# A ninth place for rotating expert chunks, the last norm's rows spread by matmuls, and the order of experts found by matmuls, in a two-block transformer kernel

## The chip, the cores and the metric

The kernel runs on one core of a Trainium2 chip. The metric is the device time of one execution in microseconds (us). Engines in what follows: PE (TensorE), PEld (its weight loads), DVE (VectorE), ACT (ScalarE), POOL (GpSimd), SP (SyncE, which issues most DMA transfers).

## The reference, cut to what matters

Two transformer blocks for 256 tokens of width 1024, in float32. The first (attention beside retention, then a dense feed-forward) is not touched. The second adds 16 meta tokens, runs a gated delta rule beside a stick-breaking attention, merges the two branches, and ends in a mixture of experts and a layer norm:

```python
def second_block(...):
    ...
    mix = hybrid_mixer(h, ...)                    # ends in merged @ w_out
    h = layer_norm_2(ALPHA * h + mix, ln1_g, ln1_b)
    ffn = hierarchical_moe(h, ...)
    h = layer_norm_2(ALPHA * h + ffn, ln2_g, ln2_b)
    return h[:, N_META:]

def hierarchical_moe(h, ...):                     # 4 groups of 8 experts, EXPERT_FF = 256
    g_idx = argmax(softmax(t @ router_group_w + b)); ...
    top_logit, top_idx = top_k(logits of that group, 2)
    for every expert e:                           # weights 1024x256, 1024x256, 256x1024
        hid = silu(t @ w_gate[e]) * (t @ w_up[e]) * combine[:, e]
        y += hid @ w_down[e]
```

Each token uses 2 of the 32 experts, but all experts' weights are read: 48 chunks of 2 MiB.

## The kernel before, in words

Everything is one program with a hand-written order on each engine. Weights reach SBUF in chunks of 2 MiB (128 partitions x 4096 floats), numbered in the order in which they are used. `used` is a semaphore that PE raises by one for each chunk it has done with. SP walks through the chunks: for chunk n it waits until the chunk that held the same place before is used, then issues the transfer; each place has its own `landed` semaphore. Up to the experts there are 5 places in `ring`. In the expert stage (chunks 49 to 96) three more in `scr` join, SLOTS = 8: chunk 49 + m goes to place m mod 8, so it waits for chunk n-8. The first five are ring places as they come free, then the three of scr.

A gate chunk holds one expert's gate and up weights, a down chunk those of two experts. Experts 0 to 5 are fixed (chunks 49 to 57, read by number, `in_stream`), the 26 others are ranked by how many tokens chose them, and SP reads the number of the expert from the table `perm` (`in_gates`, `in_downs`). PE works through eleven groups p = 0 to 10 of 2 or 4 experts: gates 49, 50 and down 51; 52, 53, 54; 55, 56, 57; 58 to 61 with 62, 63; 64, 65, 66; 67 to 70 with 71, 72 (p = 5); 73, 74, 75 (p = 6); 76 to 79, 80, 81; 82, 83, 84; 85 to 88 with 89, 90 (p = 9); 91 to 94 with 95, 96 (p = 10). The rows of a group's tokens are gathered from DRAM (POOL, `hrows`), turned by PE (L1341), multiplied with the gates (L1361, `gate_up`), by ACT and DVE made into the hidden rows, turned (L1374), multiplied with the down weights (L1415) and added into PSUM banks 4 to 7 by a product with a selection matrix (L1383, `scatter`; L1395 the last).

`keep_warm` (L2008) is a filler: products of constants into a bank that nobody reads. In `gate_up` three of them stand between the waits for the gates of a group of four from p = 7 on (L1351 to L1354).

Chunks 57 and 58 (PIECED) take the places of 49 and 50, piece by piece as group 0's products proceed (`pieces`, L1876 to L1887; semaphore `d_mm`, L1365).

Ahead of the experts: `mgd` counts the four parts of the merged branches. Then comes the output product (w_out2, chunks 47 and 48), the norm, the router (L1289), and on DVE the choice (L1548 to L1580). PE counts tokens by expert (L1295 to L1299, `lg_mm` 2), DVE makes each token's place, `flag` (whether an expert has too many tokens, then a dense branch runs that is not the case here) and `first`, the matrix that selects group 0's rows (L1594). `rank_experts` and `order_experts` then build on DVE, on all 128 partitions and over 26x26 comparisons, the rank of each expert and `perm`.

The last norm's gain and shift are spread over the 128 partitions by a transfer of 1 MiB into `rowB[:, 1]` (`rows(5, 1, ...)` in `pool_tail`).

Of the kernel before, what the change touches and what calls it, by code (L numbers as in the profile page):

```python
# [13 lines left out]
P = 128  # L14
# [110 lines left out]
def _consts():  # L125
    n = 0
    for name, k in (("ident", P), ("ones", P), ("causal", P), ("decay", RH * P), ("xi", 2 * P), ("zeta", RH),
                    ("inv", RDK // 2), ("ucum", P), ("strict", P), ("m16", P), ("off16", P), ("causT", P),
                    ("sbmul", P), ("sbadd", P), ("ntri", P), ("neg", 1), ("tie", 8), ("iota", 3 * P), ("tid", T), ("code", NE), ("tier", NE - 6), ("rank", NE - 6), ("order", NE - 6), ("gstart", 12), ("eye32", 32)):
        CONST[name] = (n, k)  # L130
        n += k
    CONST["end"] = (n, 0)
# [8 lines left out]
def const_array():  # L141
# [39 lines left out]
    put("order", order[None, :])  # L181
    put("gstart", 1 + 128 * np.arange(12)[None, :])
# [3 lines left out]
def build(nc, IN, out):  # L186

    ctx = ExitStack()
    with ctx:
        def sb(name, shape, dt=F32):  # L190
# [10 lines left out]
            cT cTv cB_mm cB_ev eg eu hid d_mm rt_e rt_x in_rt ug R_mm E01 ex01 kvn_tr kv_ev  # L201
            gram ab rd_mm rd_v rd_a u_mm uv wv s_mm sv vn_mm vn_v o_mm o_v os orv on on_tr
# [3 lines left out]
        landed = [S.landed0, S.landed1, S.landed2, S.landed3, S.landed4, S.landed5, S.landed6, S.landed7]  # L206
# [269 lines left out]
        def pe_second(pe, mm, transposes, out_proj, keep_warm):  # L476
# [17 lines left out]
            for g, (n, m, form) in enumerate(GROUPS):  # L494
# [33 lines left out]
                if g == 20:  # L528
                    pe.wait_ge(S.ug, 1)
                    pe.wait_ge(S.nr, 8)  # L530
                    for b in range(2):
                        mm(b_(4 + b), C("ones"), M2[:, 512 * b:512 * b + 512], start=True, stop=True)
                    mm(psum[:, 6, 0:64], C("ones")[0:META, :], M2[0:META, 1024:1088], start=True, stop=True)\
                        .then_inc(S.R_mm, 1)
# [180 lines left out]
            pe.wait_ge(S.wv, 1)  # L715
# [86 lines left out]
        def act_second(act, link, ln_sqrt, act_hT):  # L802
# [78 lines left out]
            sc.copy(M3[:, 0:1024], psum[:, 3:5, :].rearrange("p a b -> p (a b)")).then_inc(S.wv, 1)  # L881
# [36 lines left out]
        def dve_second(dve, v, link, chain, residual, normalise, to_hT, proj_wait):  # L918
# [54 lines left out]
            dve.wait_ge(S.R_mm, 1)  # L973
# [220 lines left out]
        def pool_tail(pool, link, affine, rows):  # L1194
# [5 lines left out]
            rows(5, 1, S.in_row1)  # L1200
# [14 lines left out]

        lay = gnB[:, :, :].rearrange("p a b -> p (a b)")
# [26 lines left out]
        ranks, low, rise, order, key, over = (arena(408 + RANKED * n, RANKED) for n in range(6))  # L1243
        above = scr[:, 5408:5408 + RANKED * RANKED].rearrange("p (a b) -> p a b", a=RANKED)
# [27 lines left out]
        SLOTS = RING + 3  # L1272
        LATE = 6
        extra_slot = [arena(6944 + CH * n, CH) for n in range(SLOTS - RING)]
# [5 lines left out]
        def pe_experts(pe, mm, transposes, keep_warm):  # L1280
# [18 lines left out]
            mm(psum[:, 5, 2 * NE:3 * NE], C("ones"), mem[:, 1, :], start=False, stop=True).then_inc(S.lg_mm, 1)  # L1299
            keep_warm(6, 2)  # L1300
            pe.wait_ge(S.flag, 1)
            crowded = pe.value_load(flag[0:1, 0:1], min_val=0, max_val=1)
            with pe.If(crowded == 0):
                pe_gathered(pe, mm, keep_warm)
            with pe.Else():
                pe_dense(pe, mm)

        def pe_gathered(pe, mm, keep_warm):

            pe.wait_ge(S.cmb, 2)  # L1310
# [7 lines left out]
            pe.wait_ge(S.cmb, 3)  # L1318
# [26 lines left out]
            def gate_up(p):  # L1345
# [12 lines left out]
                for k in range(KD):  # L1358
                    for i, e in enumerate(group):
                        weights = ring_at(GATE[e]).rearrange("p (k n) -> p k n", k=KD)  # L1360
                        last = mm(psum[i * w:(i + 1) * w, 2, :], xg[p % 2][:, k, i * w:(i + 1) * w],  # L1361
                                  weights[:, k, :], start=(k == 0), stop=(k == KD - 1))
# [35 lines left out]
            def down(p):  # L1398
# [9 lines left out]
                for half in range(2):  # L1408
                    if p == NP - 1:
                        landed_wait(pe, DOWN[group[2 * half]])  # L1410
                    for f in range(2):
                        for i, e in enumerate(group):
                            weights = ring_at(DOWN[e]).rearrange("p (e f n) -> p e f n", e=2, f=2)
                            c = f * P + i * w
                            last = mm(psum[i * w:(i + 1) * w, half, :], turned[p % 2][:, c:c + w],  # L1415
                                      weights[:, e % 2, f, half * 512:(half + 1) * 512], start=(f == 0), stop=(f == 1))
# [5 lines left out]
            for p in range(NP):  # L1422
# [9 lines left out]
                if LATE <= p < NP - 1:  # L1432
                    add_x(p - LATE)
                    scatter(p)
            for half in range(2):
                last_scatter(half)

        def pe_dense(pe, mm):

            pe.wait_ge(S.cmb, 3)  # L1440
# [5 lines left out]
            def down(s):  # L1446
# [6 lines left out]
                w = ring_at(n).rearrange("p (e f n) -> p e f n", e=2, f=2)  # L1453
                for f in range(2):
                    for t in range(T):
                        for half in range(2):
                            last = mm(b_(4 + 2 * t + half), hid[:, s % 4, f * NT + t * P:f * NT + (t + 1) * P],
                                      w[:, e % 2, f, half * 512:(half + 1) * 512],
# [3 lines left out]
            def gate_up(s):  # L1462
# [8 lines left out]
                w = ring_at(n).rearrange("p (k w n) -> p k w n", w=2, k=KD)  # L1471
                for i in range(2):
                    for f in range(2):
                        for k in range(KD):
                            last = mm(psum[:, 2 * (e % 2) + i, f * NT:(f + 1) * NT],
                                      w[:, k, i, f * P:(f + 1) * P], hT[:, k, META:L2],
# [1423 lines left out]
```

## Time and profile before

| | |
|---|---|
| median of 3 runs | 943.24 us (942.4 to 943.26) |
| the profiled execution's own time | 943.65 us |
| its span, first to last instruction | 941.8 us |
| mean granted TensorE clock | 0.986 |
| PE / PEld busy | 889.5 / 557.5 us |
| DVE / ACT / POOL busy | 367.2 / 174.3 / 92.3 us |
| moved by DMA | 219.29 MB |

Times in rows are from the span's start. Busy time of PE is modelled from pipelined records and says little of a limit by itself. A float32 product of PE shows as two records. "idle before <-X" is how long an engine stood before an instruction and what released it. In the last quarter of the span the DMA engines are busy without a break, and PE nearly so.

### The profile page before, as it was taken

To read this page: it belongs to the slowest core of one execution; us is meant where nothing else is said; L and a number is where in the kernel's file an instruction comes from. 1 tells how busy PE (TensorE), PEld (TensorE's weight loads), DVE (VectorE), ACT (ScalarE), POOL (GpSimd) and SP (SyncE) were. 2 spreads that over 40 slices of the span, in tenths; PEclk is the share of its full clock that TensorE was granted. 3 is DMA by queue.
4 is the path that set the end of the run, shared out by engine and by line. 5 is a ranking of instruction groups with operands and counts; after the bars stand their busy time and mean duration, and the time that the engine had idled before them with its cause. 6 is when DMAs were issued, how large, how long until landed. Compare 5 with 4: busy or idle time off the path is not lost.

```text
span 941.8 us, 11299 instructions
## 1 busy us (share of the span) xinstructions
PE 889.5 (94%) x4615; PEld 557.5 (59%) x4615; DVE 367.2 (39%) x834; ACT 174.3 (19%) x359; POOL 92.3 (10%) x91
## 2 busy tenths in 40 slices
PE   6999899999999998999999999999999996899985
PEld 3446756776667663688779898577455332343331
DVE  5746816433323339363475221662256111111014
ACT  3126512100000001222241221350111100000001
POOL 0045303301101100300000000000122000000000
PEclk9999999999999999999999999999999998999998
DMA  9997847544334553033352022202597999999993
GB/s 368 431 422 280 343 182 296 196 178 179 143 137 168 200 203 134 1 136 132 127 219 103 1 90 95 85 8 90 205 393 289 386 425 423 428 420 427 424 415 135
DMA packets 22617, 219.29 MB, mean 233 GB/s; under 512 B 3297, under 2 KB 3569, under 8 KB 8098
## 3 DMA queue, kind: packets, MB, share of 16 engines
q1 hardware_dynamic: 19186, 205.76, 54.6%
q0 software_dynamic: 3376, 12.76, 3.6%
q8 instruction: 38, 0.62, 0.3%
q14 instruction: 17, 0.14, 0.0%
HBM read 219.69 MB, written 2.10 MB: 235 GB/s over the span
## 4 chain that ended last, share of the span: by engine, by line
PE 82%; DVE 7%; DMA 7%; ACT 2%; issue 1%; SPq 0%; DVEq 0%; ACTq 0%
PE psum L2276 12%; PE psum L2298 9%; PE psum L508 8%; PE psum L1361 8%; PE psum L463 6%; DMA scr<-in_gates 4%; PE psum L2064 4%; PE psum L1415 3%; PE psum L755 3%; PE psum L1383 3%; PE psum L2257 3%; PE psum L2036 3%; PE psum L582 3%; DMA ring<-in_stream 2%; PE psum L2008 2%
## 5 line engine op out<-in xcount | busy, mean ns | idle before, releaser
L2276 PE MATMUL psum<-hT,ring 128*128 128x256 f32 x512 | 115.4, 379 | 1.1 <-issue 1.1
L2276 PEld LDWEIGHTS psum<-hT,ring 128*128 128x128 f32 x512 | 97.1, 190 | 26.7 <-issue 14.2
L1361 PE MATMUL psum<-ring,hT 128*32 128x512 f32 (+1 forms) x352 | 73.8, 617 | 13.7 <-DMA scr<-in_gates 11.0
L508 PE MATMUL psum<-hT,ring 128*128 128x272 f32 x320 | 74.2, 393 | 0.0
L508 PEld LDWEIGHTS psum<-hT,ring 128*128 128x128 f32 x320 | 60.6, 190 | 12.9 <-issue 0.5
L2298 PE MATMUL psum<-scr 128*128 128x512 f32 x128 | 59.5, 592 | 0.0
L2737 DVE TENSOR_TENSOR scr<-ring 128x512 f32<-128x512 f32 x16 | 11.1, 691 | 121.6 <-PE psum L2298 121.6
L463 PE MATMUL psum<-hT,ring 128*128 128x256 f32 x256 | 57.8, 382 | 0.0
L1361 PEld LDWEIGHTS psum<-ring,hT 128*32 128x32 f32 (+1 forms) x352 | 21.5, 125 | 58.0 <-issue 55.2
L2064 PE MATMUL psum<-ring,hT 128*128 128x512 f32 (+1 forms) x128 | 53.1, 574 | 2.4 <-ACT hT L2369 2.4
L1747 DVE TENSOR_TENSOR scr<-psum,scr 128x256 f32<-128x256 f32 x11 | 4.7, 424 | 127.4 <-ACT scr L1520 127.4
L463 PEld LDWEIGHTS psum<-hT,ring 128*128 128x128 f32 x256 | 47.8, 190 | 6.6 <-issue 0.2
L2298 PE MATMUL psum<-ring,scr 128*128 128x512 f32 x96 | 46.2, 592 | 0.0
L2462 ACT ACTIVATE scr<-psum 128x256 f32<-128x256 f32 x32 | 12.3, 383 | 171.0 <-PE psum L2276 171.0
L1361 PE MATMUL psum<-scr,hT 128*32 128x512 f32 (+1 forms) x160 | 43.7, 603 | 0.0
L2064 PEld LDWEIGHTS psum<-ring,hT 128*128 128x128 f32 x128 | 24.1, 190 | 31.0 <-issue 31.0
L2298 PEld LDWEIGHTS psum<-scr 128*128 128x128 f32 x128 | 24.3, 190 | 24.6 <-issue 23.9
L2008 PE MATMUL psum<-cst 128*128 128x512 f32 x80 | 36.8, 606 | 0.0
L1383 PE MATMUL psum<-rowB,scr 128*128 128x512 f32 x80 | 36.3, 596 | 0.0
L1996 POOL TENSOR_TENSOR scr<-scr 128x256 f32<-128x256 f32 x32 | 20.5, 642 | 156.8 <-ACT scr L2462 156.8
L755 PE MATMUL psum<-scr,ring 128*128 128x256 f32 x128 | 29.1, 383 | 0.0
L582 PE MATMUL psum<-scr 128*128 128x128 f32 (+1 forms) x272 | 27.8, 253 | 0.7 <-ACT scr L870 0.4
(526 smaller groups left out, 1234.2 us busy)
## 6 DMA issues: line engine op xcount, KB each, us to landing
ring<-in_stream SPq DMA_DIRECT2D x54, 2048.0 KB, 9.2
ring<-in_gates SPq DMA_DIRECT2D x17, 2048.0 KB, 18.2
scr<-in_gates SPq DMA_DIRECT2D x8, 2048.0 KB, 23.5
ring<-in_downs SPq DMA_DIRECT2D x12, 1024.0 KB, 17.8
scr<-in_downs SPq DMA_DIRECT2D x10, 1024.0 KB, 22.8
rowB<-in_rows POOLq DMA_DIRECT2D x6, 1024.0 KB, 9.9
scr<-in_stream SPq DMA_DIRECT2D x3, 2048.0 KB, 18.4
scr<-in_downs SPq DMA_DIRECT2D x8, 512.0 KB, 15.2
```

What stands on the lines that cost most here:

```text
L463: last = mm(o, w[:, k, (i % 4) * P:(i % 4 + 1) * P], hT[:, k, META:L2], start=(k == 0), stop=(k == KD - 1))
L508: last = mm(psum[:, g % 4, 0:L2], w[:, k, m * P:(m + 1) * P], hT[:, k, :], start=(k == 0), stop=(k == KD - 1))
L582: last = mm(o, prob(lhsT, p), prob(rhs, p), start=True, stop=True)
L755: last = mm(o, w[:, k, m * P:(m + 1) * P], src[:, k, :], start=(k == 0), stop=(k == 3))
L1361: last = mm(psum[i * w:(i + 1) * w, 2, :], xg[p % 2][:, k, i * w:(i + 1) * w], weights[:, k, :], start=(k == 0), stop=(k == KD - 1))
L1383: last = mm(b_(4 + 2 * t + half), scat[p % 2][:, t * P:(t + 1) * P], yg[p % 2][:, half * 512:(half + 1) * 512], start=(p == 0), stop=False)
L1415: last = mm(psum[i * w:(i + 1) * w, half, :], turned[p % 2][:, c:c + w], weights[:, e % 2, f, half * 512:(half + 1) * 512], start=(f == 0) ...
L2008: mm(psum[:, bank, 0:width], C("ident"), C("ones", 0, 1).broadcast_to([P, width]), start=True, stop=True)
L2036: last = mm(b_(4 + 2 * t + half), src[:, k, t * P:(t + 1) * P], w[:, k, :], start=(k == 0), stop=(k == KD - 1))
L2064: return mm(psum[:, 2 * c + t, 0:b - a], hT[:, k, tok(t)], ring_at(AT["head"] + k)[:, 2048 + a:2048 + b], start=(k == 0), stop=(k == KD - 1))
L2276: last = mm(psum[:, f if f < 4 else 0, 0:NT], w[:, k, m * P:(m + 1) * P], hT[:, k, META:L2], start=(k == 0), stop=(k == KD - 1))
L2298: last = mm(b_(i), lhsT, rhs, start=(j == 0), stop=(j == FT // 2 - 1))
```

## The change

1. **A ninth place.** SLOTS is 9. The new place is made of three stretches of tables that nobody reads any more in the expert stage: `rowB[:, 1]` (4 of 8 blocks of 512 floats), constants (3), the upper half of `gnB` (1). A chunk in it is loaded by three transfers, and `block_of` finds a block of it. The places are filled in another order: three of the ring, then the three of scr and the new one, then the last two of the ring; ahead of the first scr place SP waits for `mgd` 4. Chunk n waits for n-9. The pieced chunks are 58 and 59, both read by `perm`.
2. **The last norm's rows by PE.** Since `rowB[:, 1]` is taken, the rows come as 8x256 floats into a dead constant. PE spreads them by products with a column of the identity, 256 columns at a time, two to a round into bank 3, and ACT copies each round to scr; four rounds, after group 9's scatter.
3. **Order of experts.** Two small products give the counts as a column; DVE compares on 26 partitions; two more products turn ranks into the order. `perm` is written before the branch, and the two functions on DVE go.
4. Some semaphores are merged into others that already exist, to make room for `landed8`.

```diff
-        SLOTS = RING + 3
+        WHOLE = RING + 3
+        SLOTS = WHOLE + 1
+        GAINS_AT = NP - 2
+        last_rows = arena(1824, 2, DM)
...
+        turns = freed[:RING - 2] + list(range(RING, SLOTS)) + freed[RING - 2:]
         for m in range(AT["end"] - AT["experts"]):
-            slot_of[AT["experts"] + m] = m % SLOTS if m % SLOTS >= RING else freed[m % SLOTS]
+            slot_of[AT["experts"] + m] = turns[m % SLOTS]
...
+        in_parts = ((rowB[:, 1, :, :].rearrange("p a b -> p (a b)"), 0, 4), (cst[:, 256:1792], 4, 7),
+                    (lay[:, 512:1024], 7, 8))
...
+                sp.wait_ge(S.perm, 1)
+                first_gate, second_gate = expert(gate_of[a]), expert(gate_of[b])
                 for i, (lo, hi) in enumerate(SLOT_PIECES):
...
+                if n == AT["experts"] + RING - 2:
+                    sp.wait_ge(S.mgd, 4)
                 if n < FIXED_END:
-                    sp.dma_start(ring_at(n), IN["stream"][n]).then_inc(landed[slots[n]], 16)
+                    for words, a, b in parts(n):
+                        sp.dma_start(words, IN["stream"][n][:, a * 512:b * 512]).then_inc(landed[slots[n]], 16)
...
-            rows(5, 1, S.in_row1)
+            pool.dma_start(gain_rows, IN["rows"][5].rearrange("a (b n) -> (a b) n", n=NT)).then_inc(S.in_row1, 16)
...
+            for t in range(T):
+                last = mm(psum[0:RANKED, 5, 3 * NE:3 * NE + 1], mem[:, t, FIXED:NE], C("ones", 0, 1),
+                          start=(t == 0), stop=(t == T - 1))
+            last.then_inc(S.lg_mm, 1)
             keep_warm(6, 2)
+            pe.wait_ge(S.cmb, 2)
+            number = C("num")[0:RANKED, 0:1]
+            mm(psum[0:1, 5, ORDER_AT:ORDER_AT + RANKED], number, at_rank, start=True, stop=True)
+            mm(psum[:, 5, RANKS_AT:RANKS_AT + RANKED], C("ones")[0:RANKED, :], rank_diag, start=True, stop=True)\
+                .then_inc(S.lg_mm, 1)
+
+            def last_gains(q):
+
+                pe.wait_ge(S.in_row1, 48)
+                if q:
+                    pe.wait_ge(S.gains_v, q)
+                for c in range(2):
+                    j = 2 * q + c
+                    last = mm(psum[:, 3, c * NT:(c + 1) * NT], C("ident")[0:8, j:j + 1].broadcast_to([8, P]), gain_rows,
+                              start=True, stop=True)
+                last.then_inc(S.gains, 1)
...
+                if p == GAINS_AT + 1:
+                    pe.wait_ge(S.gains_v, 4)
...
                 if LATE <= p < NP - 1:
                     add_x(p - LATE)
                     scatter(p)
+                if p == GAINS_AT:
+                    for q in range(4):
+                        last_gains(q)
...
+        def gains_out(act, q):
+            act.wait_ge(S.gains, q + 1)
+            nc.scalar.copy(last_rows[:, q // 2, q % 2 * 512:(q % 2 + 1) * 512], b_(3)).then_inc(S.gains_v, 1)
...
+            v.scalar_tensor_tensor(key, psum[:, 5, 2 * NE + FIXED:3 * NE], 64.0, C("tier"), ALU.mult, ALU.add)
+            v.scalar_tensor_tensor(key_col, psum[0:RANKED, 5, 3 * NE:3 * NE + 1], 64.0, C("num")[0:RANKED, 1:2],
+                                   ALU.mult, ALU.add)
             link(places_prefix(v, C("code")))
+            v.tensor_scalar(above, key[0:RANKED, :], key_col, None, ALU.is_gt)
             v.tensor_reduce(many, over, AX, ALU.add)
             link(places_member(v))
+            v.tensor_reduce(rank_col, above, AX, ALU.add)
             v.tensor_scalar(many, many, BIG + 0.5, None, ALU.is_gt)
             link(places_sum(v))
+            v.tensor_scalar(at_rank, C("rank")[0:RANKED, :], rank_col, None, ALU.is_equal)
+            v.tensor_scalar(rank_diag, C("ident")[0:RANKED, 0:RANKED], rank_col, None, ALU.mult).then_inc(S.cmb, 1)
...
+            dve.wait_ge(S.lg_mm, 3)
+            v.tensor_copy(ranks, psum[:, 5, RANKS_AT:RANKS_AT + RANKED])
+            order = psum[0:1, 5, ORDER_AT:ORDER_AT + RANKED]
+            link(v.tensor_tensor(low[0:1, :], C("order")[0:1, :], order, ALU.subtract))
+            v.scalar_tensor_tensor(perm[0:1, :], low[0:1, :], crowd[0:1, :], order, ALU.mult, ALU.add).then_inc(S.perm, 1)
```

SP, at the entry of the expert stage. The operand left of the arrow is the place (`ring`, `scr`, or in the kernel after `rowB`, `cst`, `gnB`). Before:

```order
L1911 DMA ring<-in_stream 128x4096 x52
L1911 DMA scr<-in_stream 128x4096 x3
L1882 DMA ring<-in_stream 128x1024
L1872 TENSOR_LOAD perm
L1872 ISA x2
L1886 ISA
L1886 DMA ring<-in_gates 128x1024
```

And now:

```order
L1966 DMA ring<-in_stream 128x4096 x50
L1966 DMA scr<-in_stream 128x4096 x3
L1966 DMA rowB<-in_stream 128x2048
L1966 DMA cst<-in_stream 128x1536
L1966 DMA gnB<-in_stream 128x512
L1966 DMA ring<-in_stream 128x4096 x2
L1925 TENSOR_LOAD perm
L1925 ISA x2
L1925 TENSOR_LOAD perm
L1925 ISA x2
```

Two ring chunks moved behind the scr places and the three-part chunk, and both reads of `perm` stand ahead of the first piece.

DVE, from the counts to the branch. Before:

```order
L1583 TENSOR_SCALAR scr<-psum 128x26
L1664 TENSOR_TENSOR scr<-psum,cst 128x64
L1585 TENSOR_REDUCE scr<-scr 128x1
L1669 TENSOR_TENSOR scr<-scr 128x64 x2
L1587 TENSOR_SCALAR scr<-scr 128x1
L1674 TENSOR_REDUCE scr<-scr 128x4
L1589 SCALAR_TENSOR_TENSOR scr<-scr 128x1
L1590 CAST flag<-scr 128x1
```

And now:

```order
L1625 SCALAR_TENSOR_TENSOR scr<-psum,cst 128x26
L1626 SCALAR_TENSOR_TENSOR scr<-psum,cst 26x1
L1704 TENSOR_TENSOR scr<-psum,cst 128x64
L1629 TENSOR_SCALAR scr<-scr 26x26
L1630 TENSOR_REDUCE scr<-scr 128x1
L1709 TENSOR_TENSOR scr<-scr 128x64 x2
L1632 TENSOR_REDUCE scr<-scr 26x1
L1633 TENSOR_SCALAR scr<-scr 128x1
L1714 TENSOR_REDUCE scr<-scr 128x4
L1635 TENSOR_SCALAR scr<-cst,scr 26x26
L1636 TENSOR_SCALAR scr<-cst,scr 26x26
L1637 SCALAR_TENSOR_TENSOR scr<-scr 128x1
```

Six small operations have come in between those that lead to `flag` and `first`.

PE, between group 9's down products and group 10's gate products. Before:

```order
L1415 MATMUL psum<-ring,scr 32x512 x16
L1334 MATMUL psum<-X,gnB 128x512
L1383 MATMUL psum<-rowB,scr 128x512 x4
L2008 MATMUL psum<-cst 128x512 x9
L1361 MATMUL psum<-ring,hT 32x512 x3
```

And now:

```order
L1446 MATMUL psum<-scr 32x512 x16
L1365 MATMUL psum<-X,gnB 128x512
L1415 MATMUL psum<-rowB,scr 128x512 x4
L1326 MATMUL psum<-cst 128x256 x8
L2070 MATMUL psum<-cst 128x512 x9
L1391 MATMUL psum<-rowB,hT 32x512
```

The eight products of 256 columns stand ahead of the filler, whose nine are still all there.

## Rows read from the trace of the kernel before

**Rows 1.** Table by stage: stretch, length, busy time by engine, granted clock, DMA share, GB/s.
```profile
660.00:680.00 20.00, 20.00 (x52) 9.05 (x51) 4.77 (x9) 0.29 (x1) 1.06 (x2) 1.00 0.54 208
700.00:720.00 20.00, 18.61 (x104) 11.00 (x102) 12.68 (x44) 2.55 (x5) 2.76 (x2) 0.91 0.72 276
740.00:900.00 160.00, 145.72 (x758) 54.24 (x758) 20.13 (x40) 13.25 (x24) 4.94 (x5) 0.97 1.01 421
```

**Rows 2.** Chain that ended last: start, length, what.
```profile
711.99 7.02 PE psum L1361 x32
...
796.69 8.39 PE psum L1361 x64
...
813.57 2.68 issue
816.25 8.78 PE psum L1361 x32
...
924.63 0.43 DVE scr L1753
...
925.11 3.64 PE psum L1415 x32
```

**Rows 3.** Waits of PE, 700 to 942 us: total, times, longest.
```profile
PE psum L1361 <- DMA scr<-in_gates: 11.0, 2, 9.0
```

**Rows 4.** Line L1916, the issues at 782.2 us (chunk 73) and 788.4 us (chunk 74).
```profile
L1916 SPq DMA_DIRECT2D ring<-in_gates x1: 338/338/338, 782.2 to 782.2; - x1
...
DMA to landing us min/median/max: 29.0/29.0/29.0
...
L1916 SPq DMA_DIRECT2D ring<-in_gates x1: 337/337/337, 788.4 to 788.4; - x1
...
DMA to landing us min/median/max: 27.7/27.7/27.7
```

**Rows 5.** Timeline of PE: start, length, instruction, idle before and its releaser.
```profile
710.14 1.84 PE L1321 MATMUL psum<-cst,scr 128*128 128x1 f32 x16
...
906.15 7.92 PE L2008 MATMUL psum<-cst 128*128 128x512 f32 x18
916.04 0.63 PE L1361 MATMUL psum<-ring,hT 128*32 128x512 f32 x3 [1.98 <-DMA scr<-in_gates]
```

**Rows 6.** Timeline of POOL.
```profile
660.76 1.06 POOL L1938 DMA_DIRECT2D rowB<-in_rows  x2 [43.77 <-DVE scr L1182]
```

**Rows 7.** Timeline of SP's queue.
```profile
687.76 2.61 SPq L1911 DMA_DIRECT2D scr<-in_stream  x3
713.89 0.33 SPq L1882 DMA_DIRECT2D ring<-in_stream  x1
716.70 0.35 SPq L1886 DMA_DIRECT2D ring<-in_gates  x1
```

**Rows 8.** The page's DMA issues: count, KB each, median us to landing.
```profile
ring<-in_downs SPq DMA_DIRECT2D x12, 1024.0 KB, 17.8
```

**Rows 9.** Timeline of DVE.
```profile
703.07 0.17 DVE L1583 TENSOR_SCALAR scr<-psum 128x26 f32<-128x26 f32 x1
703.16 0.21 DVE L1664 TENSOR_TENSOR scr<-psum,cst 128x64 f32<-128x64 f32 x1
...
715.40 0.31 DVE L1610 SCALAR_TENSOR_TENSOR perm<-scr 128x26 int32<-128x26 f32 x1
...
719.56 0.42 DVE L1747 TENSOR_TENSOR scr<-psum,scr 128x256 f32<-128x256 f32 x1 [2.71 <-ACT scr L1520]
```

**Rows 10.** Table by stage in steps of 2 us (columns as in rows 1).
```profile
816.00:818.00 2.00, 1.75 (x6) 0.76 (x8) 0.00 (x0) 0.00 (x0) 0.00 (x0) 0.62 1.03 430
...
922.00:924.00 2.00, 1.12 (x12) 0.13 (x4) 0.32 (x1) 0.38 (x1) 0.00 (x0) 1.00 0.70 264
```

**Rows 11.** The page's costliest groups: busy us, mean ns.
```profile
L2276 PE MATMUL psum<-hT,ring 128*128 128x256 f32 x512 | 115.4, 379 | 1.1 <-issue 1.1
```

**Rows 12.** Line L1513, ACT's copies of 128x512: ns min/median/max.
```profile
L1513 ACT COPY hT<-psum x11: 585/586/587, 710.3 to 896.7; 128x512 f32<-128x512 f32 x11
```

More of the change, by code:

```diff
@@ L1242, in build @@
         crowd, many = arena(908, 1), arena(909, 1)
-        ranks, low, rise, order, key, over = (arena(408 + RANKED * n, RANKED) for n in range(6))
-        above = scr[:, 5408:5408 + RANKED * RANKED].rearrange("p (a b) -> p a b", a=RANKED)
+        ranks, low, rise, key, over = (arena(408 + RANKED * n, RANKED) for n in range(5))
+        above, at_rank, rank_diag = (scr[0:RANKED, 5408 + RANKED * n:5408 + RANKED * (n + 1)] for n in range(3))
+        key_col, rank_col = scr[0:RANKED, 5488:5489], scr[0:RANKED, 5489:5490]
+        ORDER_AT, RANKS_AT = 3 * NE + 32, 4 * NE + 32
         perm = sb("perm", [P, RANKED], I32)
@@ L1434, in pe_gathered @@
                     scatter(p)
+                if p == GAINS_AT:
+                    for q in range(4):
+                        last_gains(q)
             for half in range(2):
@@ L1531, in act_gathered @@
                     .then_inc(S.yv if p < NP - 1 else S.xgv, 1)
+                if p == GAINS_AT:
+                    for q in range(4):
+                        gains_out(act, q)
         def act_dense(act):
@@ L1543, in act_dense @@
                 nc.scalar.activation(eg_s[:, e % 2, :], b_(2 * (e % 2)), ACT.Silu).then_inc(S.eg, 1)
+            for q in range(4):
+                gains_out(act, q)
         def dve_experts(dve, v, link, chain, residual, normalise):
@@ L1881, in pieces @@
                         sp.wait_ge(S.used, AT["experts"] + 2)
-                    sp.dma_start(ring_at(a)[:, lo:hi], IN["stream"][a][:, lo:hi]).then_inc(landed[slots[a]], 16)
-                    if i == 0:
-                        sp.wait_ge(S.perm, 1)
-                        g = expert(gate_of[b])
-                    sp.dma_start(ring_at(b)[:, lo:hi], IN["gates"][bass.ds(g, 1), :, lo:hi])\
-                        .then_inc(landed[slots[b]], 16)
+                    for n, g in ((a, first_gate), (b, second_gate)):
+                        sp.dma_start(ring_at(n)[:, lo:hi], IN["gates"][bass.ds(g, 1), :, lo:hi])\
+                            .then_inc(landed[slots[n]], 16)
             def last_downs():
@@ L1915, in _ @@
                 elif n in gate_of:
-                    sp.dma_start(ring_at(n), IN["gates"][bass.ds(expert(gate_of[n]), 1)]).then_inc(landed[slots[n]], 16)
+                    g = expert(gate_of[n])
+                    for words, a, b in parts(n):
+                        sp.dma_start(words, IN["gates"][bass.ds(g, 1), :, a * 512:b * 512]).then_inc(landed[slots[n]], 16)
                 else:
                     for half in range(2):
-                        sp.dma_start(ring_at(n)[:, half * (CH // 2):(half + 1) * (CH // 2)],
-                                     IN["downs"][bass.ds(expert(down_of[n] + half), 1)]).then_inc(landed[slots[n]], 16)
+                        g = expert(down_of[n] + half)
+                        for words, a, b in parts(n):
+                            lo, hi = max(a, 4 * half), min(b, 4 * half + 4)
+                            if lo < hi:
+                                sp.dma_start(words[:, (lo - a) * 512:(hi - a) * 512],
+                                             IN["downs"][bass.ds(g, 1), :, (lo - 4 * half) * 512:(hi - 4 * half) * 512])\
+                                    .then_inc(landed[slots[n]], 16)
             for n in range(2 * T):
```

94 lines of the change are left out of this document (43 added, 51 removed).

## The prediction, made before the changed kernel ran

> **What bounds the kernel now.** I read four views in this order. First the table by stage [rows 1]: from 740 us to 900 us the core's DMA share is 1.01 and the rate 421 GB/s, while PE is also nearly always busy. At 660 to 680 us the share is only 0.54. So the expert stage is a stream of 2 MiB chunks of weights at full rate. Second, the chain that ended last [rows 2]: after group 5's products (from 796.69 us) it has a stand of 2.68 us at 813.57, and from 816.25 on it is PE's own work. Third, the waits of PE: PE's gate products waited for a transfer 11.0 us in two places, 9.0 and 2.0 [rows 3]. Fourth, the landings [rows 4]: chunk 73 landed at 782.2 + 29.0 = 811.2 us, chunk 74 at 788.4 + 27.7 = 816.1 (so one step of the stream is 4.9 us), which is where PE, free since 813.57, starts group 6's gate products (816.25). The last gate, 94, landed at 916.0 [rows 5], and one step of the stream before it, at about 911.0, gate 93.
>
> The lesson is in PE's own rows at the end [rows 5]. Between 816.25 and 914.07 PE never waits for a weight (the second wait above is the one at 914). The filler of 7.92 us at 906.15 is not a wait: it is 9 matmuls in three sets of three, between the waits for the gates of the last group, and it is issued whether the gates are there or not. So the real wait for the last gate is 1.98 us [rows 5]. Stream and PE end within 2 us of each other, and making the stream alone earlier by more than that moves PE only through the place where PE last hung on the stream, chunk 74.
>
> **The ninth place.** Chunk n now waits for chunk n-9 to be used, before for n-8; the first chunk that waits for the expert stage to begin is 58 instead of 57. As everything else in the pattern is the same, chunk n+1 should land when chunk n did: 74 at 811.2 instead of 816.1, 94 at 911.0 instead of 916.0. That needs the stream to be full throughout, which [rows 1] show, and the nine chunks to be in before they are wanted: four of them now leave once the merged branches are formed (S.mgd 4, on which POOL's transfer of 660.76 us waited too [rows 6]) instead of from 687.76 on [rows 7], into a stretch that is half empty [rows 1]: from 661 us to the first gate products at 711.99 [rows 2] there is room for ten steps of 4.9 us, and the DMA share shows that not all of it is used. In SP's order of after the four are the three to scr and the one in three parts. The 1 MiB of gain and shift rows that is no longer read (half a chunk, 2.5 us of the stream) lies in the same stretch and gives nothing.
>
> The pieces of the ninth place go as three transfers (8, 6 and 2 KiB per partition) instead of one. In the trace the down chunks already go in two transfers each [rows 8] inside a stream that holds 421 GB/s, so I take 0, with at most 0.3 us for each of the five such chunks as an outer bound.
>
> **The start of the stream.** Order of experts: on PE two products of 26x1 are added ahead of the counts' signal. The nearest row is 16 records of 128x1 in 1.84 us [rows 5], 0.115 us each, so 4 records = 0.46 us. On DVE six small operations come in before `first`. Neighbours that don't wait for each other start 0.09 us apart (703.07, 703.16 [rows 9]), so 6 x 0.1 = 0.6 us. The two products that find order and ranks run on PE while DVE still compares places. Start +1.05 us; bounds: 0.5 (half hidden) and 2.0 (each linked at 0.2 us). The three operations behind `first` and the loss of the five wide ones (128x676) change nothing, since DVE stood 2.71 us before group 0's product [rows 9].
> Against this, SP sent the first piece at 713.89 but its partner only at 716.70 [rows 7], held by `perm`, written at 715.40 to 715.71 [rows 9]. Now `perm` is ready about 6 us earlier and both go at once: 0.5 MB, 1.2 us of stream, is put in a hole. DMA share at 700 to 720 us was 0.72 [rows 1]. +1.05 - 1.2 would be nothing, but the later steps hang on PE (+1.05) again and the stream is not yet backed up there; I take +0.5 for all landings (bounds -0.4 and +1.5). Chunk 74: 811.7; chunk 94: 911.5.
>
> **From chunk 74 to the last group.** Group 5's last gate lands one step earlier as well: 796.7 (PE started on it at once) - 4.9 + 0.5 = 792.3. PE needs 813.57 - 796.69 = 16.9 us for that group [rows 2], is free at 809.2, and waits till 811.7. From there to the end of group 9's scatter it took 906.15 - 816.25 = 89.9 us, so 901.6. Group 6's first products took 8.78 us where the same 32 records of group 0 take 7.02 [rows 2], at a granted clock of 0.62 over 816 to 818 us [rows 10], so partly at the 1.2 GHz level: 1.76 us lost behind a stand of 2.68. The new stand is 2.5 us, or up to 4 if group 5's own products no longer meet the low clock; if the slow stretch falls partly inside the stand, part of this comes back. I take -0.4 (bounds -1.76 and 0).
>
> **The last norm's rows by PE.** New on PE between group 9's scatter and the filler: four rounds of two 256-column products, each round waiting for ACT's copy of the last (all in bank 3). A 256-column product is two records: 115.4 us / 512 = 0.225 each [rows 11], so 0.9 us a round. ACT copies 128x512 in 0.586 us [rows 12]. Each of the two hand-overs costs 0.05 to 0.2 us (DVE 924.63 + 0.43, PE at 925.11 [rows 2]). A round is 1.7 to 1.8 us; three full ones and the last pair: 3 x 1.78 + 0.9 = 6.2 us (bounds 5.3 and 7.5). It is no filling of a gap, since the filler stays: 901.6 + 6.2 + 7.9 = 915.7, against 911.5 for the last gate. The last wait for the stream is gone and PE is what is late. 915.7 against 916.04 is -0.3; with the clock's -0.4, -0.7. Behind it the down weights are no bound: at 925.11 the chain came from DVE and not from a transfer [rows 2], and they come 4.5 us earlier. The tail (943.65 - 916.04 = 27.6 us) keeps its operations; only where the rows are read changes.
>
> Sum against the profiled execution of 943.65: 943.0. It lay 0.41 above the median of the runs, 943.24; so 942.6. Chance of this mechanism 0.42, its own range 941.0 to 943.9.
>
> **Rivals.**
> 1. The clock falls in the four rounds. They leave PE idle about 0.85 of 1.75 us for 6 us. For: PE's clock did fall behind a stand of 2.68 us [rows 2, 10]. Against: it stayed at 1.00 at 922 to 924 us, where PE was busy 1.12 of 2 us [rows 10], and the whole stand lies in one piece in group 6, in many here. Price: filler or rounds at the lower level, as group 6: +1.76, so 944.4, and with group 6 as slow as before 944.8. The Trainium skill (TensorE: Matmul & The Clock Gate, "A second HAM failure mode: psum-queue depth-cycling") says that micro-idles between groups of matmuls that cycle through PSUM can make the clock swing between its two levels; by that rule this is the outcome. The trace, with rows both ways, does not settle it. Chance 0.28.
> 2. The lead arrives whole: the rounds hide, or PE comes earlier than by chunk 74 alone. For: PE does wait there, for the last gate [rows 5]. Against: that wait is 1.98 us, and PE's 98 us since 816.25 are its own. All landings 4.45 us earlier and PE with them: 943.24 - 4.5 = 938.7. Chance 0.12.
> 3. Slower: the lead is lost before chunk 74 (three-part loads, later release, the gathers' transfers in between), but the rounds are paid. Then PE is at group 6 at 816.25 + 1.05, and the last group starts at 914.07 + 1.05 + 6.2 = 921.3 instead of 916.04: 943.24 + 5.3 = 948.5. It decides (slower than 945.13) from the point where group 6 starts after 813.9, so that 914.07 - 2.3 + 6.2 passes 916.04 + 1.9. Against: the stream has no hole after 740 us [rows 1]. Chance 0.10.
> 4. The ninth place never fills early (the four chunks go no earlier): then the stream's start is the old one; as rival 3. It is in its 0.10. The rest, 0.08, is spread on both sides.
>
> **Numbers.** 0.2% of 943.24 is 1.9 us: faster is below 941.35, slower above 945.13; that is about what a measurement can tell. Faster: rival 2's 0.12, 0.05 of the forecast (clock back whole in group 6), 0.04 of the rest: 0.21. Slower: rival 3's 0.10, 0.05 of rival 1, 0.02 of the rest: 0.17. Same: 0.62. Range 940.2 to 946.0; it leaves out rival 2's and rival 3's centres.
>
> **What would show it.** In the trace after: four of the expert chunks issued near 661 us; chunk 74 (group 6's second gate) landing at 811 to 813; the rounds as 16 records of 256 columns in about 6 us near 902 to 908; the filler behind them, and the last group's gate products starting with no wait for a transfer, at 915 to 917. The granted clock of 904 to 914 separates the forecast from rival 1. I am wrong if PE still waits for the last gate (then rounds or filler are shorter than I have them), if group 6 starts later than 813, or if the first gate products start more than 2 us later than at 711.99.

## The result

| | before | after |
|---|---|---|
| median of 5 runs | 943.24 us (941.4 to 943.87) | 946.78 us (943.66 to 947.95) |
| profiled execution: time / span | 943.65 / 941.8 us | 947.95 / 946.1 us |
| mean granted clock | 0.986 | 0.985 |
| PE / DVE / ACT / POOL busy | 889.5 / 367.2 / 174.3 / 92.3 us | 895.1 / 363.4 / 176.7 / 91.6 us |
| moved by DMA | 219.29 MB | 218.26 MB |

The ratio is 1.0042, 95% interval 1.0027 to 1.0057: 4 us slower, where 0.6 us faster was forecast, and outside the stated range of 940.2 to 946.0. One of the five runs, 943.66, is far below the other four (946.4 and more).

**The profile after.** The table by stage, against [rows 1]:

```profile
660.00:680.00 20.00, 20.00 (x54) 9.26 (x53) 5.34 (x9) 1.03 (x4) 1.18 (x3) 1.00 1.00 424
700.00:720.00 20.00, 17.92 (x112) 11.13 (x113) 8.87 (x40) 2.84 (x4) 2.08 (x2) 1.00 0.27 84
740.00:900.00 160.00, 146.66 (x769) 54.66 (x766) 20.89 (x41) 13.93 (x25) 4.94 (x5) 0.98 1.01 421
```

The stretch at 660 to 680 us, half empty before, is now full (share 1.00), and at 700 to 720 us the DMA engines have little left to do (0.27 against 0.72): the nine chunks are in early. SP's queue, against [rows 7]:

```profile
657.78 0.33 SPq L1966 DMA_DIRECT2D ring<-in_stream  x1
659.24 1.42 SPq L1966 DMA_DIRECT2D scr<-in_stream  x3
660.70 0.49 SPq L1966 DMA_DIRECT2D rowB<-in_stream  x1
661.23 0.46 SPq L1966 DMA_DIRECT2D cst<-in_stream  x1
661.74 0.46 SPq L1966 DMA_DIRECT2D gnB<-in_stream  x1
```

Four chunks leave at 659 to 662 us, the fourth in three parts. So the ninth place does what it says. The chain that ended last, against [rows 2]:

```profile
710.83 7.02 PE psum L1391 x32
...
807.71 5.01 issue
812.73 8.58 PE psum L1391 x32
...
899.09 3.60 PE psum L1415 x8
902.69 1.07 PE psum L1326 x4
903.76 0.02 issue
903.78 0.59 ACT scr L1539
904.38 0.14 issue
904.51 1.11 PE psum L1326 x4
...
908.24 2.04 PE psum L1326 x4
910.28 10.19 PE psum L2070 x18
920.47 7.13 PE psum L1391 x64
```

Group 6 starts at 812.73 instead of 816.25, so there is a lead. But not all of these 3.5 us comes from the ninth place. A stage of 14.01 us long before the experts, whose work the change leaves alone, already started 1.3 us earlier in this execution; before and after:

```profile
573.26 14.01 PE psum L463 x64
```

```profile
572.00 14.01 PE psum L465 x64
```

In the profiles of this case that start lies anywhere between 570.0 and 574.5 us. Counted from group 0's first gate product, group 6 starts after 101.9 us where it was 104.3, a lead of 2.4 us. Up to the scatter's end PE needs as long as before (902.69 - 812.73 = 90.0, before 89.9). Then the rounds: 7.6 us, of which the first pairs take 1.07 and 1.11 us and the last 2.04. The filler (L2070) takes 10.2 us where it took 7.9 [rows 5]. The last group starts at 920.47 against 916.04, without a wait for a transfer, as forecast, but 4.4 us later instead of 0.7 earlier. Table in steps of 2 us, against [rows 10]:

```profile
904.00:906.00 2.00, 1.10 (x4) 0.66 (x4) 0.00 (x0) 0.72 (x2) 0.00 (x0) 1.00 1.00 421
906.00:908.00 2.00, 1.09 (x4) 0.66 (x4) 0.00 (x0) 0.72 (x2) 0.00 (x0) 0.98 0.96 386
908.00:910.00 2.00, 1.76 (x4) 1.15 (x4) 0.00 (x0) 0.09 (x1) 0.00 (x0) 0.50 1.00 380
...
912.00:914.00 2.00, 2.00 (x4) 0.89 (x3) 0.00 (x0) 0.00 (x0) 0.00 (x0) 0.50 1.05 387
```

The granted clock (third number from the right) falls to 0.50, the 1.2 GHz level, from 908 us on: in the last round and most of the filler. From group 0 to the last group: 2.4 us gained by the lead, 7.6 paid for the rounds, 2.3 for the slow filler, less the 2.0 us that PE had stood: -2.4 + 7.6 + 2.3 - 2.0 = +5.5 (measured 5.6). Group 0 itself started 1.2 us earlier, nearly all of it from the stages ahead, so the last group starts 4.4 us later from the span's start.

### The profile page after: what moved, and what is told of

Its sections match the earlier page's. It is cut to its first block, busy times and chain, and to the rows that moved or that the text cites. A ratio compares the mean times of both kernels' runs of the same rounds, so it can differ in the third digit from the quotient of the medians.

```text
span 946.1 us, 11386 instructions
## 1 busy us (share of the span) xinstructions
PE 895.1 (95%) x4639; PEld 561.9 (59%) x4639; DVE 363.4 (38%) x835; ACT 176.7 (19%) x363; POOL 91.6 (10%) x91
## 2 busy tenths in 40 slices
DMA packets 23946, 218.26 MB, mean 231 GB/s; under 512 B 3465, under 2 KB 3745, under 8 KB 9554
## 4 chain that ended last, share of the span: by engine, by line
PE 85%; DVE 6%; DMA 4%; ACT 2%; issue 2%; SPq 0%; DVEq 0%; ACTq 0%
PE psum L2338 12%; PE psum L2360 9%; PE psum L510 8%; PE psum L1391 8%; PE psum L465 6%; PE psum L2126 6%; PE psum L2070 3%; PE psum L1446 3%; PE psum L757 3%; PE psum L1415 3%; DMA gnB<-in_gates 3%; PE psum L2319 3%; PE psum L2098 3%; PE psum L584 3%; PE psum L2112 1%
## 5 line engine op out<-in xcount | busy, mean ns | idle before, releaser
L2070 PE MATMUL psum<-cst 128*128 128x512 f32 x80 | 38.4, 628 | 0.0
L1391 PE MATMUL psum<-scr,hT 128*32 128x512 f32 (+1 forms) x96 | 35.3, 594 | 0.0
## 6 DMA issues: line engine op xcount, KB each, us to landing
scr<-in_gates SPq DMA_DIRECT2D x4, 2048.0 KB, 25.8
```

Of the source, the lines that this page charges most:

```text
L2070: mm(psum[:, bank, 0:width], C("ident"), C("ones", 0, 1).broadcast_to([P, width]), start=True, stop=True)
```

## The experiments

In the table and below, "G0" is the start of group 0's gate products and "G10" that of the last group's, in the profiled execution; the distance between them leaves out what the start of the program does. Before: 204.05 (a second profile: 204.17), after: 209.64 (a second: 209.82). Ratios are each to the runs of the kernel before on the same chip.

| kernel | ratio [95%] | G0 to G10, us |
|---|---|---|
| e1 no rounds | 0.9966 [0.9949, 0.9983] | 200.27 |
| e2 no filler in the last group | 0.9992 [0.9975, 1.0010] | 200.92 |
| e3 filled rounds | 1.0039 [1.0018, 1.0059] | 206.82 |
| e4 rounds in four banks | 1.0011 [0.9990, 1.0032] | 206.16 |
| e5 filled rounds, no filler in the last group | 0.9998 [0.9983, 1.0013] | 199.86 |
| e6 order of experts alone | 1.0027 [1.0012, 1.0042] | 204.59 |
| e7 order and rounds, eight places | 1.0105 [1.0086, 1.0124] | 210.65 |
| e8 as e5, no fillers at all | 0.9986 [0.9970, 1.0002] | 200.50 |
| e9 four banks, 128 rows | 0.9989 [0.9976, 1.0003] | 203.10 |
| e10 as e9, no filler in the last group | 1.0002 [0.9985, 1.0020] | 200.44 |
| e11 as e10, fillers at the start | 0.9992 [0.9975, 1.0008] | 201.57 |
| e12 order alone, fillers at the start | 1.0007 [0.9995, 1.0020] | 204.33 |
| e13 all of it, shorter filler | 0.9959 [0.9947, 0.9971] | 200.51 |
| e14 the changed kernel again | 1.0068 [1.0042, 1.0094] | 209.82 |
| e15 the kernel before again | 0.9992 [0.9975, 1.0010] | 204.17 |
| e16 changed kernel, fillers at the start | 1.0070 [1.0048, 1.0093] | 212.56 |

### Taking the rounds or the filler away

**e1.** The rounds out; shown is PE's part, ACT's four copies and the waits for them go too:

```diff
-                if p == GAINS_AT:
-                    for q in range(4):
-                        last_gains(q)
```

> The changed kernel without the four rounds of PE and ACT that spread the last norm's rows (the last norm then takes whatever lies in that buffer, so gain and shift are left out). Theory A (PE's own work ahead of the last group is what cost the time): group 9's scatter ends near 902.6 us, the filler near 910.5, the last gate lands near 911.4 and the last group starts there, 4.6 us earlier than before's 916.04, so 939 us and a clear gain. Rival B (the ninth place itself costs: three-part transfers, other order of loads): still 945 us or more.

939.36 us. The ninth place without the rounds gains: ratio 0.9966. The last group hangs on its last gate:

```profile
895.86 18.05 DMA ring<-in_gates
913.91 0.04 issue
913.95 7.20 PE psum L1391 x64
```

200.3 us after G0 (713.68), 3.8 less than before: once nothing else stands in PE's way, the last group hangs on the stream, and the stream's lead is 3.8 us, a little less than the step of 4.9 us that the prediction started from. Rival B falls.

**e2.** The rounds stay, the last group's filler goes (`LATE < p < NP - 1` in `gate_up`).

> The changed kernel without the filler between the gates of the last group alone (9 matmuls); the rounds stay. Theory A: rounds end near 910.2 us, the last group starts when gate 94 lands, near 911.4, its products partly at the low clock (up to 1.8 us more): 939 to 941 us. Rival C (the stream of weights is the bound, the filler only fills its wait): no change, 947 us.

942.43 us. G10 is again on the landing, 200.92. The last group's products took 9.17 us instead of 7.1, since the clock stood low from 909.5 to 919.7 us. The median is 1.4 us above the 939 to 941 that I expected. The filler was on the path, so rival C (947 us) falls; and it has its use, since without it the products pay.

**e7.** Eight places in the old order, with the rounds:

```diff
-        SLOTS = WHOLE + 1
+        SLOTS = WHOLE
...
-        turns = freed[:RING - 2] + list(range(RING, SLOTS)) + freed[RING - 2:]
+        turns = freed + list(range(RING, SLOTS))
```

> Order of experts by PE and the rounds, but eight places in the old order. Theory A: without the lead the rounds (7.6 us) and the slow filler (+2.4) stand against the 2.0 us that PE waited: 8 us over the kernel with the order alone, 951 to 952 us. Rival G (the rounds hide in the wait for the last gate): as the kernel with the order alone, at most 2 us more.

951.53 us, 6.3 above e6 (945.26), which has the same without the rounds, where I expected 8; on the path G0 to G10 it is 6.1. The rounds do not hide, and rival G falls. e7 less the changed kernel is the ninth place's worth: 951.53 against 946.78 in another measurement, ratios 1.0105 and 1.0042 (e14: 1.0068), so 3.5 to 6 us.

**e6.** As e7, and the last norm's rows by the 1 MiB transfer again; only the order of experts is left.

> Only the order of experts by PE, with eight places in the old order and the last norm's rows by the 1 MiB transfer as before. Theory E (this part costs at the start, where the clock falls longer in many executions: 704 to 711 us in two profiles instead of 704 to 707): 2 to 3 us over before, and the low stretch near 704 us is 6.8 us long. Rival F (its cost is the +1.05 us forecast, partly given back by the earlier perm): 0 to 1 us over before, 943.5 us.

945.26 us, ratio 1.0027: 2.5 us, by the bound of rival F too much. In its profile, taken of an execution of 946.62 us, the clock was at the low level from 702.7 to 709.5 us, and the first 32 products took 5.89 us instead of 4.49 before:

```profile
704.00:708.00 4.00, 3.89 (x18) 3.45 (x18) 2.76 (x7) 0.00 (x0) 0.00 (x0) 0.50 1.03 441
```

That stretch puts G0 140.9 us behind the stage of 14.01 us, 2.1 to 2.5 more than in the two profiles of the kernel before. It is not the whole excess of that execution: the last group's products also met the low clock (917.7 to 921.2 us), behind stands of 1.0 and 2.0 us, and took 8.89 us instead of 7.2.

### What lets the clock fall

**e3.** A product of 384 columns over 128 rows in the gap behind each of the first three rounds:

```diff
+                if keep:
+                    mm(psum[:, 2, 0:384], C("ident"), C("ones", 0, 1).broadcast_to([P, 384]), start=True, stop=True)
```

> The changed kernel with one filler product of 384 columns behind each of the first three rounds, in the gap in which PE stood. Theory A2 (of the 4.4 us, about 3.3 are the clock that fell in the rounds): the clock stays at 1.00, rounds 6.5 us, filler 7.9, the last group starts near 917.0, 944.5 us in all executions. Rival D (the fall comes of something else, or costs nothing on the path): 947 to 948 us as the changed kernel.

In the profile as theory A2 has it: no low clock between 820 and 939 us, rounds 6.8 us, filler 8.0, G0 to G10 206.8 (after: 209.6). The median, 947.45, does not show that gain: ratio 1.0039, where 944.5 us, or 1.0015, was expected. The twelve runs lie between 941 and 950 us. The profiled execution itself took 948.32 us although its rounds ran at the full clock: the 2.8 us gained there were lost ahead of G0, 2.1 to a low clock at 704 to 711 us (G0 140.9 us behind the stage of 14.01 us) and 1.1 in the stages before it. So a single time says little of the rounds. Of the three profiles with filled rounds, e3 and e8 held the clock through the rounds and e5 had it down from 908 us on; how often filling half the time is enough stays open.

**e4.** Four banks, PE does not wait between rounds:

```diff
-                if q:
+                if q and bank is None:
                     pe.wait_ge(S.gains_v, q)
...
+        GAIN_BANKS = (2, 3, 0, 1)
```

> The changed kernel with the four rounds in four PSUM banks (2, 3, 0, 1) instead of all in bank 3, so that PE doesn't wait for ACT between them; PE waits for the first copy ahead of the filler. Theory A: the eight products take 3.6 to 4 us instead of 7.6, the clock stays, filler 7.9, the last group starts near 914.3 us: 941.8 us. If ACT's waits were not the cost (rival D): 946 us or more.

944.0 us, where I expected 941.8. Shorter than the changed kernel, but not for the reason I had. The rounds take 4.8 us, and the filler still 10.2:

```profile
902.00:904.00 2.00, 2.00 (x11) 1.68 (x10) 0.00 (x0) 1.17 (x2) 0.00 (x0) 0.95 0.96 409
904.00:906.00 2.00, 2.00 (x6) 1.22 (x4) 0.00 (x0) 0.59 (x1) 0.00 (x0) 0.50 0.94 390
906.00:908.00 2.00, 2.00 (x3) 0.84 (x3) 0.00 (x0) 0.59 (x1) 0.00 (x0) 0.50 1.05 417
```

PE is busy 2.00 of 2 us, and from about 903.8 us on the clock is at 0.50. Standing between rounds is not what makes it fall here.

**e9.** e4 with products over all 128 rows:

```diff
-C("ident")[0:8, j:j + 1].broadcast_to([8, P]), gain_rows,
+C("ident")[:, j:j + 1].broadcast_to([P, P]), cst[:, CONST["sbadd"][0]:CONST["sbadd"][0] + NT],
```

> The kernel with the rounds in four banks, its eight products now over 128 rows of both operands instead of 8 (the identity's column is zero in the added rows, so the result is the same; columns and count are the same). Theory I (products over 8 rows don't keep the clock up, however dense): the clock stays at 1.00 through rounds and filler, rounds 3.7 us, filler 7.9 (10.2 with 8 rows), the last group starts 203.9 us after group 0 (206.2 with 8 rows); about 2 us under the kernel with 8 rows. Rival J (the number of rows does not matter): the clock falls as there, same time.

941.03 us. PE's rows at the place:

```profile
909.60 3.62 PE L1327 MATMUL psum<-cst 128*128 128x256 f32 x16
913.06 7.92 PE L2073 MATMUL psum<-cst 128*128 128x512 f32 x18
```

against e4's:

```profile
901.39 4.86 PE L1327 MATMUL psum<-cst 8*128 8x256 f32 x16
906.17 10.22 PE L2072 MATMUL psum<-cst 128*128 128x512 f32 x18
```

The same 16 records of 256 columns: 3.62 instead of 4.86 us, and the filler 7.92 instead of 10.22. The clock stayed at 1.00:

```profile
910.00:912.00 2.00, 2.00 (x11) 1.74 (x11) 0.00 (x0) 1.05 (x2) 0.00 (x0) 1.00 1.04 439
912.00:914.00 2.00, 2.00 (x9) 1.39 (x8) 0.00 (x0) 1.28 (x3) 0.00 (x0) 1.00 0.94 379
```

In the kernels only the number of rows differs. G0 to G10 is 3.06 us shorter, and the medians 3.0 us (different chips; ratios 0.9989 and 1.0011, whose intervals overlap). Theory I holds in the profiles, rival J falls there. The support is uneven: the dense products over 8 rows were profiled once (e4), those over 128 rows four times (e9, e10, e11, e13), each time in 3.62 us.

The Trainium skill (TensorE: Matmul & The Clock Gate, "A second HAM failure mode: psum-queue depth-cycling") lays such swings to micro-idles between groups of matmuls that cycle through banks of PSUM. e4, without such idles, had the low clock all the same, so in e4 that rule is not what decided. For the changed kernel, which has both the idles and the 8 rows, no run tells them apart: none has rounds that wait for ACT and 128 rows.

### Which filler is worth its time

**e5.** e3 and e2 together.

> The changed kernel with filler products of 384 columns in the gaps of the first three rounds, and without the filler between the last group's gates. Theory A: the clock holds through the rounds, PE is free near 7 us after the scatter, before the last gate lands; the last group starts on that landing, about 200.3 us after group 0's first gate product (before: 204.05; changed: 209.6) and runs at the full clock: 3.8 us under before, 939.3 us. Rival C (the ninth place gives no lead that lasts): 943 us or more.

942.64 us, where I expected 939.3. G10 on the landing (199.86), but 8.53 us of products instead of 7.1 and a later end: behind the start of the last group the execution took 27.1 us, against 25.6 to 25.8 where the clock was up. The rest of the expected 3.8 us I did not find in its profile, which at 940.92 was among its faster executions.

**e8.** e5 without any filler from group 7 on (`keep_warm` in `gate_up` removed).

> As the kernel with filled rounds and no filler in the last group, and the fillers of groups 7 and 9 left out too. Theory A: PE is then far ahead and waits for transfers in each group; the last group still starts on the landing of gate 94, 200 us after group 0's first product, so no gain over the kernel that keeps them, and up to 2 us lost where the clock falls behind the stands: 939.5 to 941.5 us. Rival H (the fillers of groups 7 and 9 are on the path too): 937 us or less.

942.02 us, just above the 939.5 to 941.5 expected. Group starts at 838.51 and 882.93 us with products of 8.86 and 8.88 us, and the last 9.39:

```profile
892.41 19.88 DMA ring<-in_gates
912.64 9.39 PE psum L1391 x64
```

The last group waits for its gate as in e5, and the products pay 2 us. The four rounds ran at the full clock here (a pair 1.13 us); it fell from about 911 us on, behind PE's stand of 3.55 us. Rival H falls: with nine places the stream is the bound, and the fillers of groups 7 and 9 cost nothing.

**e10.** e9 without the last group's filler.

> As e9 and without the filler between the last group's gates. PE is free 3.7 us after the scatter and stands about 5 us for gate 94. Theory A: the last group starts on the landing, 200 us after group 0; its products meet the low clock behind the stand (up to 2 us): 940 to 942 us.

942.36 us, no better than e9 (941.03) though G10 is 2.7 us earlier: products 9.31 us.

### The start, and all of it

**e11 and e12.** Fillers at the start:

```diff
-            keep_warm(6, 5)
+            keep_warm(6, 6)
...
                 .then_inc(S.lg_mm, 1)
+            keep_warm(6, 2, 256)
```

> As e10, and at the start one more filler product (512 columns) in the wait for the choice and two of 256 columns behind the two products that find the order. Theory E (the clock falls for 6.8 us near 704 us in many executions of the new order of experts, 2 us each): no fall there, group 0's products start 138.2 to 138.9 us after the stage of 14.01 us before: 2 us under e10. Rival F (the order of experts costs by its own instructions): no change against e10.

> The order of experts by PE alone (eight places, rows by transfer) with the same fillers at the start. Theory E: falls back from 2.7 us over before to 0 to 1 us over before. Rival F: stays at 2 to 3 us over before.

e12: 942.95 us, ratio 1.0007 where e6 had 1.0027, clock 1.00 at the place where e6 had 0.50:

```profile
704.00:708.00 4.00, 3.80 (x30) 3.49 (x30) 3.02 (x11) 0.00 (x0) 0.00 (x0) 1.00 1.03 441
```

e11: 942.0 against e10's 942.36, no difference that can be told, and not the 2 us expected. Its clock was low from 693.3 to 696.8 us instead, and G0 came 140.1 us behind the stage of 14.01 us, not 138.2 to 138.9.

**e15, e14, e16.**

> The kernel before unchanged. Theory E (the fall of 6.8 us near 704 us belongs to the new order): its low stretch there is at most 3.4 us and group 0 starts about 138.7 us after the stage of 14.01 us. Rival: 6.8 us and about 140.9, as in the kernels with the new order; then the order is not the cause. Same time as before.

> The changed kernel unchanged, beside the others on one chip. 3 to 5 us over before; in its profile the low clock from about 908 us on in the rounds and the filler, and near 704 us in about every second execution.

> The changed kernel with the fillers at the start alone; the rounds over 8 rows in one bank and the slow filler stay. Theory E: 2 to 2.7 us under the changed kernel, 1 to 2 us over before. Rival F: no change against the changed kernel.

e15: the low stretch near the start lies at 696.4 to 699.8 us, 3.4 us long, and G0 comes 138.4 us after the stage of 14.01 us. e14: 948.58 us, 6.4 us over the kernel before by its ratio and so more than the 3 to 5 expected; clock low in rounds and filler (906.0 to 916.2), but no fall near 704 us and 138.8. e16 did not gain: 949.93, ratio 1.0070, where e14 has 1.0068. Its rounds had the low clock too (907.1 to 917.3). So theory E holds for the order alone (e6 against e12, intervals that overlap a little) and not as a part of the changed kernel's loss. How often each kernel meets that fall can't be told from one or two profiles each. Taken together, of the twelve profiles with the new order and no fillers at the start four have G0 at 140.9 us (e2, e3, e6, e8, low clock near 704 us), and of the four with the fillers none (e11 has 140.1 by its stretch at 693 us); that leans to theory E and does not settle it.

**e13.** Nine places, rounds in four banks over 128 rows, fillers at the start, and a shorter filler in the last group:

```diff
-                        keep_warm(2, 3)
+                        keep_warm(2, 3 if p < NP - 1 else 2)
```

> Ninth place; rounds in four banks over 128 rows; two products instead of three in each of the three fillers between the last group's gates; fillers at the start. Theory: rounds 3.7 us and 5.3 us of filler end when gate 94 lands, with the clock up: the last group starts 200.5 us after group 0 and runs at the full clock: 3 to 4 us under before, 939 us. Rival: as e9, 1 us under before, if the stand for the gate lets the clock fall anyway.

938.52 us, ratio 0.9959 [0.9947, 0.9971]: 4 us faster than the kernel before, and about 8 to 10 faster than the changed one. PE at the place:

```profile
900.92 3.62 PE L1328 MATMUL psum<-cst 128*128 128x256 f32 x16
904.37 5.33 PE L2074 MATMUL psum<-cst 128*128 128x512 f32 x12
910.21 0.62 PE L1394 MATMUL psum<-rowB,hT 128*32 128x512 f32 x1 [0.51 <-DMA ring<-in_gates]
```

Rounds and filler end 0.5 us ahead of the last gate, and the products behind it run in 7.20 us.

## Why the prediction was wrong

The direction was missed by one term of the sum, and a second one besides, part of which an earlier start of the profiled execution hid.

- **"The last norm's rows by PE", 6.2 us and "filler 7.9".** This step failed, in its size. Without the clock a round is 1.87 us (902.62, 904.51, 906.38: two hand-overs of 0.02 and 0.14, a copy of 0.59, a pair of 1.1, where 1.7 to 1.8 was forecast with a pair at 0.9), three and a pair 6.7. The clock made 7.6 of it and 10.2 of the filler: 3.7 us over the forecast together. That this could happen was rival 1; it had a chance of 0.28 and a price of 1.76, copied from group 6. The price in this place was 3.2 (0.9 in the rounds and 2.3 in the filler): the low stretch was 6.8 us long and fell wholly into work on the path, where group 6's was half that. And it was the rule, not the exception: all five profiles with the rounds as the changed kernel has them (after, e2, e7, e14, e16) had the low clock in the last round at the latest. Of the other four with products over 8 rows, e4 and e5 had it in the rounds, e3 and e8 did not. I took "idle for half the time" for the reason and set [rows 10] against it. e4 and e9 show another: with eight products over 8 rows the clock fell though PE was busy without a break, with the same over 128 rows it did not. What part the stands have in the changed kernel, beside the rows, is not shown. Of the rows shown before none had such a product, so [rows 11] gave their duration and nothing on the clock.
- **"Chunk 74: 811.7".** Group 6 started at 812.73, 1.0 us later. By luck that looks small. The execution was 1.3 us ahead from the stages before, and the start of the experts cost 0.9 us less than forecast (below); from G0 on, group 6 came after 101.9 us where 98.7 was forecast, 3.2 us late. The rule was that a chunk lands when the one ahead of it did before. Chunks 69 and 70 kept it: they landed at 784.3 and 790.0 us, 1.4 to 1.7 us ahead of it, which is about the head start. Chunk 71 had lost that, and chunk 73, one of those in three parts, landed 1.4 us behind it, at 807.7 us and 6.3 us after chunk 72. Its later fellows in three parts, 82 and 91, landed 5.1 us after their forerunners, so the three parts alone are not shown as the cause. What took the time was not tried.
- **The clock's -0.4 in group 6** did not come: 8.58 us against 8.78, with PE standing 6.9 us ahead of it instead of the 2.5 to 4 forecast, since chunk 74 was late and group 5, which met no low clock, took 15.5 us instead of 16.9.
- **The start, +1.05 and then +0.5.** On G0 the two profiles show 138.83 and 138.82 us behind the stage ahead, before 138.73 and 138.37: 0.1 to 0.5 us more, less than forecast. As a part by itself (e6) the order cost 2.5 us. The difference may be the low clock near 704 us, which was not in the changed kernel's two profiles, and the one in e6's last group.
- **"It is no filling of a gap, since the filler stays" and "PE is what is late".** Right: e7 shows 6.1 us for the rounds on the path, e1 that without them the last gate is the bound.
- **"Chunk n+1 should land when chunk n did."** Right in mechanism: the last gate's lead is 3.8 us from G0 on in e1, where 4.5 was forecast from the span's start and 5.6 from a G0 that was to be 1.05 later.
- **The tail** was right: from G10 to the end of the span 25.6 us after, 25.8 before.

The sum: 943.0 for the profiled execution, +1.0 (chunk 74: 3.2 late from G0 on, less 0.9 at the start and 1.3 of chance), +0.2 (group 6), +1.4 (rounds), +2.3 (filler) = 947.9; measured 947.95.

## What to carry to other kernels

When a transfer stream and an engine both end within 2 us, a lead in the stream is worth what the engine can take of it: look what the engine issues unconditionally ahead of the wait (here a filler of 7.9 us), for anything put beside it adds to it. A filler has to be cut to the gap that is left; too long it is work, and missing it costs 2 us of slow products. And a product with few rows may be no small thing for the clock: giving the eight dense products the full 128 rows cost nothing and took 3 us off the path from G0 to G10, in one profile against another.

## What the runs showed of the hardware that was not expected

- Eight float32 products of 256 columns over 8 rows, back to back (PE busy 2.00 of 2 us): the granted clock fell to 0.50 while they ran and stayed there for 6.8 us, most of it in the filler behind them (e4); with the same over 128 rows it stayed at 1.00 (e9).
- A low clock can last 13.7 us in a stage where 14 of the 18 profiles have none. e7, at 602 to 614 us, against the kernel before in the same stage, whose code is the same:

```profile
602.00:614.00 12.00, 11.22 (x54) 5.72 (x53) 6.13 (x26) 0.59 (x2) 0.00 (x0) 0.50 0.00 1
```

```profile
602.00:614.00 12.00, 11.22 (x87) 7.16 (x86) 9.19 (x35) 3.52 (x6) 0.00 (x0) 1.00 0.01 1
```

It puts G0 4.5 us later (143.4 us behind the stage ahead instead of 138.8) and was in the profiles of e1, e7, e9 and e10. It is one reason why a kernel's runs spread over 5 us and more, and why the path between two events of one profile tells more here than a single time.
- Three transfers of 8, 6 and 2 KiB per partition for a chunk did not lower the rate: 421 GB/s from 740 to 900 us before and after. It does not follow that each chunk lands on time; see chunk 74 above.
